# Swapping the order of two memory projections that fill gaps in an attention loop

## The reference, cut to what matters

```python
# first layer
a_out = dsa_attention(q, k, v, qi, ki, wi)      # 4 blocks of 128 queries x 8 heads
u = causal_dwconv(ga * sigmoid(gg), conv_b_w, conv_b_b)          # 31 taps
b_out = silu(layernorm(u, ln_b_g, ln_b_b))
x = x + concatenate([a_out, b_out]) @ w_out
hq = rmsnorm(x, norm_cross_g)
m = rmsnorm(mem, norm_mem_g)                    # 256 memory tokens
qc = hq @ w_q_cross
kc = m @ w_k_cross                              # key projection of the memory
vc = m @ w_v_cross                              # value projection of the memory
oc = softmax(qc kc^T * scale) vc                # cross attention, after w_out
```

## Time and profile before

| | |
|---|---|
| time, median of 3 runs | 1380.87 us (1379.4 to 1382.4) |
| the profiled execution: span from its first to its last instruction | 1377.8 us |
| median less span: what lies around the span, about | 3.1 us |
| mean granted clock of TensorE over the span | 0.992 |
| loop of the 35 steps, first logits to `mean` | 120.8 to 227.7 us of the span |

### The profile page before, as it was taken

The page is one execution under the profiler, slowest core; times in us unless marked ns, Lnnn a source line. Parts: engine busy times, 40 slices in busy tenths (PEclk is TensorE's granted clock), DMA queues, the critical chain, the costliest instruction groups (busy, mean ns, idle before and its releaser), DMA issues. The chain is left out here.

```text
span 1377.8 us, 18053 instructions
## 1 busy us (share of the span) xinstructions
PE 1335.7 (97%) x6189; PEld 1083.1 (79%) x6189; DVE 787.6 (57%) x1097; ACT 550.0 (40%) x860; POOL 611.5 (44%) x299
## 2 busy tenths in 40 slices
PE   8998989999999999999999999899999999999997
PEld 7787767887678888888888777678688888888887
DVE  7788896642457777777434588765543333332231
ACT  5444676542353233232232354545443223223322
POOL 4597873332244444444434533122244444444441
PEclk9999999999999999999999999999999999999999
DMA  6122320221122232233232222011122222233222
GB/s 229 60 92 92 108 78 31 92 78 61 46 92 92 91 105 93 91 105 102 98 105 86 86 80 87 31 54 54 59 86 101 91 100 98 91 100 106 101 86 81
DMA packets 31875, 121.19 MB, mean 88 GB/s; under 512 B 3536, under 2 KB 3664, under 8 KB 31568
## 3 DMA queue, kind: packets, MB, share of 16 engines
q1 hardware_dynamic: 31536, 119.81, 25.7%
q10 hardware_dynamic: 288, 0.69, 0.1%
HBM read 118.40 MB, written 2.10 MB: 87 GB/s over the span
## 5 line engine op out<-in xcount | busy, mean ns | idle before, releaser
L619 POOL TENSOR_TENSOR weights_low<-weights_raw,weights_high 128x1024 fp32r<-128x1024 f32 (+1 forms) x204 | 525.8, 2578 | 733.1 <-ACT weights_high L697 732.9
L697 ACT CAST weights_high<-weights_raw 128x1024 fp32r<-128x1024 f32 (+1 forms) x202 | 222.0, 1099 | 506.7 <-PE acc L1730 474.3
L1730 PE MATMUL acc<-a_high,weights_high 128*128 128x512 f32 x976 | 389.6, 399 | 1.8 <-DVE a_low L1392 1.1
L1730 PE MATMUL acc<-a_high,weights_low 128*128 128x512 f32 x976 | 380.9, 390 | 0.0
L1730 PE MATMUL acc<-a_low,weights_high 128*128 128x512 f32 x976 | 380.4, 390 | 0.0
L1730 PEld LDWEIGHTS acc<-a_high,weights_high 128*128 128x128 f32 x976 | 183.5, 188 | 44.2 <-issue 3.8
L1730 PEld LDWEIGHTS acc<-a_low,weights_high 128*128 128x128 f32 x976 | 183.6, 188 | 39.0 <-issue 2.6
L1730 PEld LDWEIGHTS acc<-a_high,weights_low 128*128 128x128 f32 x976 | 183.3, 188 | 38.8
L1202 DVE TENSOR_TENSOR residual<-acc,residual 128x512 f32<-128x512 f32 (+1 forms) x63 | 43.3, 687 | 174.3 <-PE acc L1730 129.8
L1730 PE MATMUL acc<-h_high,weights_high 128*128 128x512 f32 x330 | 129.1, 391 | 0.0
L1730 PE MATMUL acc<-h_high,weights_low 128*128 128x512 f32 x330 | 128.6, 390 | 0.0
(11 more groups left out here) (384 smaller groups left out, 1955.4 us busy)
## 6 DMA issues: line engine op xcount, KB each, us to landing
weights_raw<-w SPq DMA_DIRECT2D x172, 512.0 KB, 3.2
weights_raw<-w SPq DMA_DIRECT2D x32, 704.0 KB, 4.0
residual<-xT SPq DMA_DIRECT2D x8, 256.0 KB, 6.7
out<-y_tok SPq DMA_DIRECT2D x4, 512.0 KB, 3.1
mem_raw<-memT SPq DMA_DIRECT2D x1, 1024.0 KB, 5.3
mem_tok<-mem SPq DMA_DIRECT2D x1, 1024.0 KB, 7.4
lru_weights<-blockdiag ACTq DMA_DIRECT2D x1, 512.0 KB, 3.3
sine<-positions SPq DMA_DIRECT2D x1, 256.0 KB, 7.3
```

The costliest lines, as they stand in the source:

```text
L619: g.tensor_tensor(weights_low[:, s, 0:cols], weights_raw[:, s, 0:cols], weights_high[:, s, 0:cols].bitcast(F32), ALU.subtract).then_inc(we ...
L697: a.copy(weights_high[:, s, 0:cols], weights_raw[:, s, 0:cols]).then_inc(weight_high, 1)
L1730: last = t_.matmul(acc[:, bank, 0:cols], w[:, s, wide], x_[:, k0 + k, 0:cols], start=start and k == opens and n == 0, stop=stop and k == c ...
```

## The change

The value projection `vc` becomes fillers 0 to 7 and the key projection `kc` fillers 8 to 15; the weights are laid out in that order. The pieces are spread anew: before, 22 of the 31 pieces lie in steps 0 to 16 and 9 in steps 17 to 34; now 15 and 16. No operation is added or removed.

```diff
-GEMMS = (("in", 16), ("kc", 8), ("vc", 8), ("out", 8), ...
+GEMMS = (("in", 16), ("vc", 8), ("kc", 8), ("out", 8), ...
...
-        FILLS_AT = (2, 1, 2, 1, 2, 1, 2, 1, 1, 1, 2, 1, 1, 1, 1, 1, 1, 1, 0, 1, 1, 0, 1, 0,
-                    1, 0, 1, 0, 0, 1, 0, 0, 1, 0, 1)
+        FILLS_AT = (1, 1, 1, 1, 1, 1, 1, 1, 1, 1, 1, 0, 1, 1, 0, 1, 1, 1, 1, 1, 1, 1, 1, 1,
+                    1, 1, 0, 1, 1, 0, 1, 1, 1, 1, 1)
...
             def fill_ends(n):
-                q = CHUNK["kc"] + n
+                q = CHUNK["vc"] + n
                 high_next(q // 2, q % 2)
-                if n >= KB and n % 4 == 3:
+                if n < KB and n % 4 == 3:
                     act.wait_ge(chunk_done, q + 1)
                     act.wait_ge(mem_factor, 1)
                     for b in range(MB):
-                        at_ = (n - KB) // 4 * T
+                        at_ = n // 4 * T
...
-                elif what == "fill" and n[2] == KB and j < KB:
-                    dve.wait_ge(chunk_done, CHUNK["kc"] + j + 1)
-                    v.tensor_tensor(kcT[:, j], acc[:, j % 2, 0:MB * P], mem_row[:], ALU.mult
+                elif what == "fill" and n[2] == KB and j >= KB:
+                    dve.wait_ge(chunk_done, CHUNK["vc"] + j + 1)
+                    v.tensor_tensor(kcT[:, j - KB], acc[:, j % 2, 0:MB * P], mem_row[:], ALU.mult
...
             def memory(n, k, end):
-                q = CHUNK["kc"] + n
+                q = CHUNK["vc"] + n
...
-                if n < KB:
+                if n >= KB:
                     if k == 0:
-                        free(n % 2, TILE["kc"] // 2 + n // 2)
+                        free(n % 2, TILE["kc"] // 2 + (n - KB) // 2)
                     chunk(q // 2, q % 2, end, q % 2, M, cols=MB * P, first=k)
                     return
                 part = n % 4
                 if part == 0 and k == 0:
                     for b in range(MB):
-                        free(b, TILE["vc"] // 2 + (n - KB) // 4)
+                        free(b, TILE["vc"] // 2 + n // 4)
```

More of the change, by code:

```diff
@@ L35 @@
 TWO_PI = (6.28125, 0.0019350051879882812, 3.0199159819567e-07)
-GEMMS = (("in", 16), ("kc", 8), ("vc", 8), ("out", 8), ("qc", 8), ("oc", 8), ("ffn", 2 * FB),
+GEMMS = (("in", 16), ("vc", 8), ("kc", 8), ("out", 8), ("qc", 8), ("oc", 8), ("ffn", 2 * FB),
          ("down", 16), ("in2", 20), ("out2", 8), ("ffn2", 2 * FB), ("down2", 16))
@@ L638, in _ @@
                 elif what == "fill" and n[2] == KB:
-                    low_after(CHUNK["kc"] + j)
+                    low_after(CHUNK["vc"] + j)
                 elif what == "first" and n[1] == 1 and n[3] == 4:
@@ L2288 @@
     w8 = np.concatenate([
-        _column_blocks(w_in, starts), _column_blocks(a["w_k_cross"][0], d),
-        _row_pairs(a["w_v_cross"][0]), out1,
+        _column_blocks(w_in, starts), _row_pairs(a["w_v_cross"][0]),
+        _column_blocks(a["w_k_cross"][0], d), out1,
         _column_blocks(a["w_q_cross"][0], d), oc, pairs[0],
```

## The result

| | before | after |
|---|---|---|
| time, median of 21 runs each | 1380.52 us (1378.95 to 1382.4) | 1381.59 us (1379.47 to 1384.49) |
| ratio after to before | | 1.0013, 95% interval 1.0007 to 1.0019 |
| profiled execution: time, span | span 1377.8 us | 1382.9 us, span 1381.1 us |
| step 17 on PE | 175.69 us | 169.62 us |
| `mean` on PE | 227.69 us | 228.20 us |

The change costs 0.13%, 1.1 us of the median. That lies within the 0.2% named ahead as no change; 1381.4 us was predicted. The page of after answers to the earlier trace rows with the same shares.

The account below looks back on a forecast made before the run. PE, busy 97% of the span, was taken as the bound. Early -8.3, late +7.4 and clock +1.4 gave +0.5 us: span 1378.3 us, plus 3.1 us around it 1381.4 us; range 1377.3 to 1384.1 us.

Parts of the forecast that it names:

- The early stretch: Loop up to the start of step 17, bound by DVE: 42.3 for 50.6 us, -8.3 us (-10.1 to -6.5).
- removed from DVE: the three waits, 6.15 us: Early steps: DVE's waits for key tiles, 3.97 + 1.80 + 0.38 us, vanish as the tiles move late.
- The pause of step 7: PE stands still some 3 us for ACT's read-outs of step 6; DVE waits 1.0 us before step 8's mask.
- The first piece: Loop start: the value projection opens both banks, so it waits for ACT's copy; 0.25 us added, 0 to 1.4.
- The late stretch: Step 17 to the loop's end, bound by PE: seven more pieces, 59.4 for 52.0 us, +7.4 us (+4.4 to +9.8).
- The gap at step 17: Step 17's piece opens the banks of step 16's read-outs and waits on ACT's chain: 1.2 us.
- The clock: After step 7's pause the granted clock falls to 0.50 once: +1.4 us, 0 if it holds, +3.4 if twice.
- the slower rival's sign: Clock falls more than once, steps 7 to 17: second stretch at 0.50 between 140 and 180 us; 1384.3 us, chance 0.15.
- `mean` carries through one for one: After the loop PE follows one chain, so a shift of the start of `mean` is the shift of the time.
- POOL: Rival, early steps: POOL's low parts and adds hold PE up by 2 us at step 17; 1383.4 us, chance 0.09.
- That pieces only fill holes: Faster rival: no new gap late (+4.4), early -8.3, clock holds; -3.9 us, span 1377.0 us, chance 0.12.
- That is all there is to win: Whole loop: only PE's idle time can be won, 6.85 us early and 5.43 us late.

Follow-up runs that it names:

- e1: The kernel before (key projection first) with only the changed kernel's table of pieces; median 1380.34 us, ratio to before 1.0005.
- e2: The changed kernel (value projection first) with the table of pieces of the kernel before; median 1383.02 us, ratio to before 1.0027.
- e9: The changed kernel with low parts for the first twelve pairs formed for half the columns only, relieving POOL; median 1382.53 us, ratio to before 1.0014.
- e3: The changed kernel with ACT's two read-outs ahead of the rounding of the next chunk; median 1380.75 us, ratio to before 1.0005.
- e10: The changed kernel with one piece in each of steps 0 to 30 and ACT's read-outs ahead of the rounding; median 1373.91 us, ratio to before 0.9952.
- e6: The kernel before (key projection first) with one piece in each of steps 0 to 30, none after; median 1372.78 us, ratio to before 0.9952.
- e5: The changed kernel with two of three passes in the last four key chunks; median 1377.78 us, ratio to before 0.9982.
- e11: The changed kernel with another table, no piece in the step right behind each of the two read-outs; median 1375.93 us, ratio to before 0.9956.
- e7: The changed kernel (value projection first) with one piece in each of steps 0 to 30, none after; median 1377.98 us, ratio to before 0.9987.
- e4: The changed kernel with small extra matmuls in PE's pauses of steps 7 and 14; median 1381.13 us, ratio to before 1.0008.

## Why the prediction was right, and where it wasn't

**The early stretch.** Predicted -8.3 us and +1.4 us for the clock, together -6.9; measured -6.07. The size was nearly right and the reason wrong, which is luck. The sum's first term, "removed from DVE: the three waits, 6.15 us", was put down to the key tiles leaving. By e1 the waits go with the tiles in place, by e2 they turn into waits for logits when only the tiles go. The spread gains 9.1 us, and the order then gives 3.1 us back (41.45 to 44.52 us, with two falls of the clock in the latter and none in the former).

**The pause of step 7.** Predicted some 3 us near 142 us, measured 2.78 us at 141.70 us; DVE's wait ahead of step 8 was put at 1.0 us and came out at 2.01 us. From the waiting piece to the mask of step 8 I had 1.4 + 0.8 = 2.2 us; it was 3.20 us in after, with the clock at 0.50, and 143.70 - 141.29 = 2.41 us in e9, where the clock stayed at 1.00. e3 and e10 show the chain on ACT to be the cause: a rounding less ahead of the read-outs is 0.96 us less pause.

**The first piece.** Put at 0.25 us, kept to 1.4: PE waited 1.90 us for ACT's copy, and DVE then only 0.42 us for the rotation behind it.

**The late stretch.** Predicted 56.4 us of PE and 3.0 us of gaps; measured 56.48 and 2.10 us. That seven pieces cost 7 x 1.4 us held well (9.91 us of busy time). The gap at step 17 was 0.47 us, not 1.2: step 16's read-outs were ready in time. A step without a piece had 1.19 us, near the 1.3 us taken. The stretch came out 0.82 us shorter than predicted and the early one 0.83 us longer, so the two misses cancel in `mean`. By the rule of the Trainium skill ("Perfetto Trace Analysis", Identifying the Most-Contended Engine) on the weight loads' share the pieces would have fitted at no cost; the trace disagrees, since the stretch grew by 6.58 us. The section names MFU, the rate of arithmetic against the peak, beside that share; it was not worked out here.

**The clock.** Predicted one stretch at 0.50, near 143 us; there were two, from 143 to 147 us and from 163.5 to 167 us, the second behind the 2.17 us of step 14. So the slower rival's sign did show, and most of its mechanism. But the time was not its 1384.3 us: DVE, not PE, was busy nearly all of the second stretch (0.96 of the us at 165) and waited 0.75 us behind it, and the second read-out cost 0.47 us.

**What the time hides.** `mean` came where the sum put it, but that the time lies 0.2 us from the prediction is luck: two more errors cancelled. The 3.1 us around the span were 1.8 us in the profiled execution: a median less the span of another execution also holds the difference of their clocks. And the span was 2.8 us above my 1378.3 us, all of it behind `mean`, from clock stretches in the second layer. In the execution of the median, 1381.59 us, the span was 1379.7 us: 1.4 us too much in the span, and 1.9 us around it for 3.1. That `mean` carries through one for one holds for the work, not for the clock. From `mean` to the end it is 1149.9 to 1150.3 us in six of the thirteen profiled executions, and 1151.3 to 1155.1 us in the others. One place parts most of them: some 546 us behind `mean` (the row of after from 770 us) the clock fell in six of the seven longer ones and in none of the six shorter ones. The seventh is e3, with a long fall some 645 us behind `mean`. What makes these falls more or less frequent is open, and so is why e1's 2.9 us at `mean` did not show in its time.

**The other rivals.** POOL: not up to step 7, by e9; behind it nothing shows in the time, within 1.5 us. That pieces only fill holes: true early (e6 holds two more there for nothing), not late (e5).

**What was missed.** "That is all there is to win", 12.28 us of idle time, held nearly: e6 has 4.55 + 1.39 = 5.94 us left, and `mean` 7.25 us earlier. Left out was what the clock costs inside PE's busy time, 97.15 us before and 95.43 us in e6 from the first piece to `mean`. The change had taken one good half, no double pieces early, and paid for it by pushing seven pieces, not five, past step 17, with a piece in each of the last four steps.

## What to carry to other kernels

Filler work is free only where the filled engine idles: count the idle time of each stretch apart, and price every piece beyond it at its full length (here 1.4 us). When a buffer that takes two banks is read out, try the read-out first in its engine's list, or a step without a user of those banks behind it: e10 and e11 did so, and their time is not told from that of e6. Change order and spread one at a time: here e6's spread alone gave 0.48%, and the same spread with the new order (e7) 0.13%.

## What the runs showed of the hardware

A pause of the same kind may or may not lower TensorE's granted clock. The 1.90 us ahead of the first value piece left it at 1.00 in after; in e3 (and in e4, e5 and e10), behind the same 1.90 us, it went to 0.50, the 1.2 GHz level, and the same matmul of 512 columns went from 0.40 to 0.63 us within one piece of e3:

```profile
120.42 0.40 PE L1852 MATMUL acc<-weights_low,m_high 128*128 128x512 f32 x1
120.66 0.54 PE L1852 MATMUL acc<-weights_high,m_high 128*128 128x512 f32 x1
120.99 0.63 PE L1852 MATMUL acc<-weights_high,m_low 128*128 128x512 f32 x1
```

In e9 it stayed at 1.00 behind 3.29 us. So one profile shows one draw: kernels that their ratios don't tell apart can have their `mean` 2.0 us apart, as after and e9 have, and only runs in number compare them.
